# Three row gathers of a mixture-of-experts layer, each issued as two transfers of unequal size

## The reference, cut to what matters

```python
idx = jnp.take_along_axis(cand_i, pos, axis=-1)
g = jax.nn.softmax(best_s, axis=-1)
...
act = jax.nn.gelu(jnp.einsum('nd,nhkd->nhk', xb, u_table[ib]).astype(F32)) * gb
return jnp.einsum('nhk,nhkd->nd', act.astype(xb.dtype), v_table[ib])
```

## Time and profile before

| | |
|---|---|
| median of 3 runs | 834.13 us (831.78 to 834.73) |
| the profiled execution, its own time | 834.09 us |
| its span, first to last instruction | 832.3 us |
| busy: PE, DVE, POOL, ACT | 701.8, 592.0, 364.0, 345.2 us |
| moved in all | 321.74 MB, mean 387 GB/s |
| moved by the gathers (queue 0) | 268.45 MB |

### The profile page before, as it was taken

How to read it: one execution, slowest core, us unless ns; L and a number is a source line. 1 busy time by engine, 2 the same in 40 slices (tenths; PEclk the granted TensorE clock), 3 DMA queues, 4 the chain that set the end, 5 groups by cost and what they waited for, 6 DMA issues and landing times.

```text
span 832.3 us, 10365 instructions
## 1 busy us (share of the span) xinstructions
PE 701.8 (84%) x3383; PEld 346.3 (42%) x3383; DVE 592.0 (71%) x1290; ACT 345.2 (41%) x1032; POOL 364.0 (44%) x318
## 2 busy tenths in 40 slices
PE   3898999999988999899879788778777777777875
PEld 0475656656434466667424232223222222222221
DVE  7899613677995659858898757777687478744546
ACT  4634441445466343343354433353334333433332
POOL 3029800244435473345455544536444444545410
PEclk9999999999999999899999999999999999999999
DMA  9958696989999999999999999999999999999992
GB/s 349 418 175 287 229 392 263 348 305 419 406 424 368 425 422 422 422 421 422 422 420 423 422 421 423 422 422 422 422 422 424 421 422 424 421 422 424 422 422 100
DMA packets 50414, 321.74 MB, mean 387 GB/s; under 512 B 9964, under 2 KB 10668, under 8 KB 12472
## 3 DMA queue, kind: packets, MB, share of 16 engines
q0 software_dynamic: 37008, 268.45, 78.1%
q1 hardware_dynamic: 12984, 52.44, 16.3%
q10 hardware_dynamic: 368, 0.18, 0.1%
HBM read 318.77 MB, written 1.23 MB: 384 GB/s over the span
## 4 chain that ended last, share of the span: by engine, by line
DMA 41%; PE 33%; DVE 14%; issue 4%; ACT 4%; POOL 3%; SPq 1%; POOLq 0%; ACTq 0%; DVEq 0%
DMA mem<-uv_table,small 36%; PE psum L879 12%; DVE mem L1913 5%; PE psum L812 5%; PE psum L783 3%; DMA spare_page<-uv_table,small 3%; POOL mem L1556 2%; DMA mem<-w_mod 2%; PE psum L601 1%; PE psum L579 1%; PE psum L528 1%; DVE mem L1863 1%; PE psum L709 1%; PE psum L682 1%; ACT mem L1277 1%
## 5 line engine op out<-in xcount | busy, mean ns | idle before, releaser
L879 PE MATMUL psum<-mem 128*128 128x512 f32 x862 | 425.7, 624 | 96.2 <-ACT mem L1277 92.5
L1556 POOL DMA_INDIRECT mem<-uv_table,small x231 | 274.0, 1186 | 295.1 <-PE psum L879 244.0
L1913 DVE CUSTOM_DVE_ANT_0 mem<-mem,h 128x1024 f32<-128x1024 f32 x232 | 282.9, 1226 | 148.3 <-DMA mem<-uv_table,small 137.1
L879 PEld LDWEIGHTS psum<-mem 128*128 128x128 f32 x862 | 153.7, 194 | 337.5 <-ACT mem L1277 204.4
L1266 ACT ACTIVATE small<-small 128x1 f32<-128x1 f32 x252 | 50.9, 202 | 283.5 <-DVE small L1913 273.9
L1277 ACT ACTIVATE mem<-consts,small 128x128 f32<-128x128 f32 x238 | 95.6, 402 | 8.0
L1271 ACT ACTIVATE small<-small 128x1 f32<-128x1 f32 x256 | 75.4, 294 | 26.4 <-DVEq L1898 3.0
L1556 POOL DMA_INDIRECT spare_page<-uv_table,small x24 | 31.0, 1290 | 36.3 <-PE psum L879 20.2
L879 PE MATMUL psum<-spare_page,mem 128*128 128x512 f32 x88 | 42.4, 604 | 4.0 <-ACT mem L1277 3.9
L1913 DVE CUSTOM_DVE_ANT_0 spare_page<-spare_page,h 128x1024 f32<-128x1024 f32 x24 | 29.4, 1225 | 16.9 <-DMA spare_page<-uv_table,small 16.2
L812 PEld LDWEIGHTS psum<-hT,mem 128*128 128x128 f32 x288 | 34.1, 192 | 5.7 <-issue 5.7
(11 more groups left out here) (258 smaller groups left out, 735.0 us busy)
## 6 DMA issues: line engine op xcount, KB each, us to landing
mem<-w_mod SPq DMA_DIRECT2D x24, 1024.0 KB, 8.5
mem<-w_query SPq DMA_DIRECT2D x6, 1024.0 KB, 9.0
mem<-w_out SPq DMA_DIRECT2D x4, 1024.0 KB, 7.6
mem<-uv_table,small POOLq DMA_INDIRECT x233, 27.1
mem<-w_in_u SPq DMA_DIRECT2D x2, 1024.0 KB, 14.9
late<-w_query SPq DMA_DIRECT2D x2, 1024.0 KB, 6.9
mem<-w_in_qkv SPq DMA_DIRECT2D x2, 1008.0 KB, 12.0
mem<-w_ukv SPq DMA_DIRECT2D x1, 1024.0 KB, 11.3
```

The costliest lines, as they stand in the source:

```text
L879: mm = pe.matmul(bank(f"acc_{g}_{half}"), diag[:, pick % DEEP, :], row_of(pick)[:, D + 512 * half:D + 512 * half + 512], start=first, stop ...
L1556: pool.indirect_dma_start(row_of(pick), None, uv_table, bass.IndirectOffsetOnAxis(ap=idx[:, pick:pick + 1] if pick else first_idx, axis=0) ...
L1913: dve.tensor_tensor_reduce(out=row[:, 0:D], in0=row[:, 0:D], in1=h[:, pick // PICKS, :], scale=1.0, scalar=0.0, op0=ALU.mult, op1=ALU.add, ...
```

## The change

Picks 182, 214 and 230 are gathered by two transfers instead of one: the last 2 (24, 8) lines first, then the first 126 (104, 120). An indirect transfer takes its line numbers from partition 0 upward, so the numbers of the last lines are first copied from `idx` to the new little tile `end_idx` by a small transfer on SP's queue; POOL waits for that one. Both transfers of a pick raise the same `row_landed`, so `ROW_USE` counts such a pick twice. Nothing of the computation changes.

```diff
+SPLIT = {182: 2, 214: 24, 230: 8}
...
-        count[page_] = count.get(page_, 0) + 1
+        count[page_] = count.get(page_, 0) + 1 + (pick in SPLIT)
...
+        end_idx = part(4).bitcast(U32)
...
             sp.dma_start(fnb, final_norm.to_broadcast([P, D])).then_inc(fn_in, 16)
-            sp.wait_ge(y_out_ready, 1)
-            sp.dma_start(y_prompt, h[:, 0, :]).then_inc(stored, 16)
+            for at_, (pick, n_) in enumerate(SPLIT.items()):
+                if pick == 230:
+                    sp.wait_ge(y_out_ready, 1)
+                    sp.dma_start(y_prompt, h[:, 0, :]).then_inc(stored, 16)
+                sp.wait_ge(idx_ready, pick // BATCH + 1)
+                sp.dma_start(end_idx[0:n_, at_:at_ + 1], idx[P - n_:P, pick:pick + 1]).then_inc(end_idx_in[pick], 16)
...
+                if pick in SPLIT:
+                    at_, n_ = list(SPLIT).index(pick), SPLIT[pick]
+                    pool.wait_ge(end_idx_in[pick], 16)
+                    pool.indirect_dma_start(row_of(pick)[P - n_:P, :], None, uv_table,
+                                            bass.IndirectOffsetOnAxis(ap=end_idx[0:n_, at_:at_ + 1], axis=0)).then_inc(row_landed[ROW[pick]], 16)
+                    pool.indirect_dma_start(row_of(pick)[0:P - n_, :], None, uv_table,
+                                            bass.IndirectOffsetOnAxis(ap=idx[0:P - n_, pick:pick + 1], axis=0)).then_inc(row_landed[ROW[pick]], 16)
+                    return
```

More of the change, by code:

```diff
@@ L173, in layer @@
         consts = sb("consts", [P, sum(n for _, n in CONSTS)])
-        small = sb("small", [P, 821])
+        small = sb("small", [P, 825])
         psum = ctx.enter_context(nc.psum_tensor("psum", [P, 8, 512], F32))
@@ L352, in layer @@
         ckv_stored, ssm_stored = sem("ckv_stored"), sem("ssm_stored")
+        end_idx_in = {pick: sem(f"end_idx{pick}_in") for pick in SPLIT}
         low_meant, high_squared = sem("low_meant"), sem("high_squared")
```

## The result

The changed kernel takes 858.89 us (median of 4 runs, 858.20 to 859.37), the kernel before in the same comparison 834.03 (4 runs, 831.78 to 834.73). The ratio is 1.0296, 95% interval 1.0277 to 1.0316. It is slower by 24.9 us, and the forecast of 830.5 was wrong, its range to 840 too.

A forecast was written before the change was run, and what follows sets the result against it. The prediction took the expert stage to be bound by the gathers' bytes, its end by the last DMA engine. It summed 834.1 - 3.6 + 0 = 830.5 us, range 828.8 to 840.

The forecast's parts named there:

- The transfers bound the stage: Expert stage: bound by the gathers' bytes, all 16 engines busy at 422 GB/s, 2.48 us a pick.
- The deal: Split gathers: lines go in equal shares to the largest number of engines, at most 16, that divides them.
- the numbering of the engines in the sum: Split gathers: each transfer starts at the engine after the last one's; last engine taken as number 0, second as 1.
- the wait for `end_idx`: POOL before each split gather: number copies land early, margins of 53 and 38 us, so the wait is free.
- the later store: The y_prompt store goes some 4 us later, 190 us before the end, at no cost.
- POOL's issues: Three more gather issues of 0.94 to 1.14 us on POOL, hidden by 27 us of queue: nothing.
- The term -3.6: End of the gathers: fewer lines on the two last engines end them 3.45 to 3.7 us earlier, taken as 3.6.
- The last engine's lag: End of the gathers: last engine 5.8 us behind the mean, likely from instruction packets, returning in the same place.
- The ceiling of 5.8 us: End of the gathers: the most any change could gain, by perfect dealing of lines among engines.
- Rival C: Split gathers: engines writing the same partitions share one engine's rate, no relief; 836 to 841.5 us, chance 0.28.
- A: The forecast itself, last engine relieved by the uneven shares: 830.5 us, range 829 to 832, chance 0.50.
- The remark against C: Transfers in the expert stage: share of 1.01 at 422 GB/s leaves open whether engine or memory side sets the rate.

The follow-up runs named there:

- half8b: Kernel before with eight picks, 200 to 207, each gathered as upper and lower 64 partitions: 857.42 us against 834.22.
- stride8: Kernel before with picks 200 to 207 each gathered as even and odd partitions, 64 lines each: 835.08 us against 833.48.
- prime182: Changed kernel with only pick 182 split, into 15 and 113 lines: 875.47 us against 833.57 for the kernel before.
- copies: Changed kernel with number copies and POOL's waits kept, but the three picks gathered whole: 833.09 us against 833.49 for the kernel before.
- columns: Changed kernel with the three picks in two transfers of all 128 partitions and half a line, no SP copies: 834.37 us against 833.49 before.
- even182: Changed kernel with only pick 182 split, into 16 and 112 lines: 839.09 us against 833.94 for the kernel before.
- only182: Changed kernel with only pick 182 split, 2 and 126 lines, its copy issued ahead of the y_prompt store: 839.86 us against 833.57 before.
- one182: Changed kernel with only pick 182 split, 2 and 126 lines, its copy behind the y_prompt store, so POOL stood: 839.73 us against 833.49 before.
- even16: Changed kernel with all three picks cut into 16 and 112 lines: 854.04 us against 833.49 for the kernel before.

## Why the prediction was wrong

**What happens.** In a whole gather each engine takes eight lines and, as all runs have it, writes eight partitions of its own; all 16 have their full rate. Cut 64/64 by halves, all 16 engines write into one half of the partitions, where only half of these groups lie; the rate is 228 to 240 GB/s (`half8b`). Cut by every second partition they reach all groups, and the rate stays at 422 to 424 (`stride8`). Cut 2/126 the shares are 9 each for 14 engines, by the deal assumed, and most lines fall into the group of another engine. Two engines that write to one group together get about one engine's rate: 0.62 us a line for each of a pair in `prime182`, 0.554 in the mean of `half8b`, against 0.310. One engine alone gets its full rate at 26 partitions (`prime182`). That rules out the engine and the size of the transfer, and, since `half8b` and `stride8` fetch the same lines of the table, the reading side; it leaves the way into the partitions.

Which eight partitions share a way I have not measured. The Trainium skill states it (page "SBUF — State Buffer", section "Door 1: The DMA port swizzle"): 16 ports for eight partitions each, of which partitions 0 to 63 reach only eight and 64 to 127 the other eight. By it `half8b` loses and `stride8`, whose transfers reach all 16, need not; the runs agree. By its table a port's eight are not a run of eight but two blocks of four, 32 apart. The step at every fourth line in `prime182` fits the blocks of four; a run of eight would want it at every eighth line. No run tests the two maps against each other.

**The transfers bound the stage: right.** Each hole in the rate came back as time. But the prediction read the share of 1.01 as engines at full use; the same share stands at half the rate.

**The deal: right in the one point that was tested.** `prime182` shows the 113 lines on one engine, as the largest divisor up to 16 says (the Trainium skill, page "DMA: Bandwidth & Descriptors", section "Why a DMA increments its semaphore by 16 and not by 1"; the rounded-up shares that it allows for some direct copies did not occur in this gather). That transfers start behind one another, and so the numbering of the engines in the sum, was not tested.

**Free were, as said,** the wait for `end_idx`, the later store and the copies (`copies`, -0.4 with 0 inside the interval), POOL's issues and the second transfer (`columns`, +0.9 with 0 well inside the interval). The store of `y_prompt` went out at 641.09 us, 8.5 later than before and not some 4.

**The term -3.6 failed, in the step "With 0.310 us a line that is -3.7, -1.55, +0.93, -1.2, +0.6 us", from which it has the ends at 817.4 and 817.35.** It prices a displaced line at the line time of undisturbed engines, and takes a line off an engine for time off that engine. The runs show 0.585 to 0.705 us a line in the holes, and the last engine ended at about 845.7 in place of 817.4: 4.2 us further behind the mean than before, and not 3.6 earlier. And `even182`, which relieves nobody, costs 5.2 us, about what `only182` costs, where engines 0 and 1 carry 14 lines less between them: no relief to be seen. The last engine's lag in the trace of `only182` is 5.0 us, within what the uncut kernels show. The ceiling of 5.8 us stands untested as a gain: only the dry queue of `one182` brought the lag down, to 1.1 us, and it paid for that with a stop. Which engine is the last, and whether the packets of instructions make the lag, no run shows.

**Rival C was the mechanism, and its price was wrong by a factor of three.** The step was "the price is up to one pick time for each split, 3 x 2.48 = 7.4 us". It took it that only the lines of the split gather are slow. The runs show 4.5 to 7.8 us of lost rate for each split and 6.3 to 9.8 in all. The likely reason, argued and not shown by itself: the engines are up to 9 us apart, so a displaced line meets a neighbour that is still at an older pick or at a later one, and that neighbour's lines, of whole gathers, are slowed too; each waits in its own order, so the hold-up is handed on, through a hole of 10 to 15 us. Two observations speak for it: after the dry queue of `one182`, with the engines together, the same split lost about 1.4 us of rate only; and eight split picks in a row cost 23.2 us, 2.9 each, close to the one pick time that I had assumed, where single ones cost 5.2 to 9.8. The entering and leaving of a displaced gather costs most. Whether 214 and 230 cost more than 182 is open: 9.1 and 9.8 against 6.3 us, with intervals that overlap, though their holes in the changed kernel are deeper too (5.7 and 7.8 us of rate against 4.5). A reason would be that, by the deal assumed, 24/104 takes 12 + 13 engines and 8/120 takes 8 + 15, no multiples of 16, so that all whole gathers behind them start at another engine; no run tested that, and `even16`, where nothing shifts, still loses 20.5 against 3 x 5.2.

**The chances.** C had 0.28 and A 0.50. The remark against C was that a share of 1.01 at 422 GB/s leaves open which side sets the rate. That is no evidence against it, and C should have been the likelier: if an engine and its way into the partitions have about the same rate, every displaced line costs something, in each of three splits, against a gain of at most 5.8 us that a guess about one engine's number had to win.

## What to carry to other kernels

A gather's shape decides which engine writes which partitions, and when the DMA queues are full, every gather in flight should have the same map. Cut along the line it was free here; cut by every second partition eight picks cost 1.6 us (0.4 to 3.0). Cut off a few partitions, even two, and each cut costs 5 to 10 us here. Don't value a line moved to another engine by the engine's time alone. Look for a share near 1 with a falling rate: here it meant that engines waited on each other. And mind the divisors of a line count: 113 lines went through one engine.

## What the runs showed that I had not expected

- One engine of 16 out of place takes the total from 422 to 380 GB/s (`prime182`, 644 to 660 us), more than the one sixteenth that a pair at half rate would cost.
- A stop of POOL of 28 us, in a stage that issues a gather every 2.5 us, cost 6.2 us together with a split (`one182`): the 27 us of queue covered most of it, and the engines were together again behind it, 1.1 us of lag at the end.
- The engines' share reads 1.02 in the worst holes. Busy time says nothing of progress.
